# Order in which the moving columns are walked, and their places in SBUF against the weights

## What is computed

```
h = concat(meta, x)                                   # 272 tokens
for l in 0, 1:                                        # first block
    h += 0.5 * swiglu(rmsnorm(h), gate, up, down)     # 1024 -> 2816 -> 1024
    h += hybrid_mixer(rmsnorm(h))                     # w_in 1024 -> 4608, then attention, a 31-tap conv, w_out
    h += 0.5 * swiglu(rmsnorm(h), gate, up, down)
h = rmsnorm(h)[16:]                                   # 256 tokens
for l in 0, 1:                                        # second block
    h += 0.5 * swiglu(rms(h), ...)
    h += differential_attention(rms(h)) if l == 0 else retention(rms(h))
    h += 0.5 * swiglu(rms(h), ...)
```

## Time and profile before

| | |
|---|---|
| median of 2 runs | 2207.22 us |
| the profiled execution | 2210.91 us |
| its span (first to last instruction) | 2209.1 us |
| PE busy | 2198.0 us (99%), 18114 matmuls |
| PEld (weight loads) busy | 2180.8 us (99%), 18114 loads |
| DVE busy | 1602.4 us (73%) |
| ACT busy | 1276.6 us (58%) |
| chain that ended last | PE 98%, ACT 1%, DVE 1% |
| read from HBM | 384.18 MB, 174 GB/s over the span |

### The profile page before, as it was taken

How to read it: one execution, slowest core, us unless ns; L and a number is a source line. 1 busy time by engine, 2 the same in 40 slices (tenths; PEclk the granted TensorE clock), 3 DMA queues, 4 the chain that set the end, 5 groups by cost and what they waited for, 6 DMA issues and landing times.

```text
span 2209.1 us, 48942 instructions
## 1 busy us (share of the span) xinstructions
PE 2198.0 (99%) x18114; PEld 2180.8 (99%) x18114; DVE 1602.4 (73%) x2450; ACT 1276.6 (58%) x1988; POOL 282.1 (13%) x328
## 2 busy tenths in 40 slices
PE   8999999999999999999999999999999999999999
PEld 8999999999999999999999999999999999999999
DVE  6655997665566579887768767888768766777775
ACT  6444786544444368766546646876556645565662
POOL 0001661100100136220020012010010010101000
PEclk9999999999999999999999999999999999999999
DMA  6555435555455544455555555355556645445553
GB/s 229 174 188 165 159 122 170 167 171 195 155 173 183 179 161 144 144 185 186 190 169 193 195 183 163 124 178 194 195 181 200 219 162 177 161 162 194 188 200 124
DMA packets 100408, 386.68 MB, mean 175 GB/s; under 512 B 11312, under 2 KB 12464, under 8 KB 100304
## 3 DMA queue, kind: packets, MB, share of 16 engines
q1 hardware_dynamic: 99648, 383.89, 52.2%
q0 software_dynamic: 368, 1.26, 0.2%
q10 hardware_dynamic: 288, 0.12, 0.0%
HBM read 384.18 MB, written 1.05 MB: 174 GB/s over the span
## 4 chain that ended last, share of the span: by engine, by line
PE 98%; ACT 1%; DVE 1%; issue 0%; DMA 0%; ACTq 0%
PE bank L387 16%; PE bank L389 15%; PE bank L388 15%; PE bank L395 15%; PE bank L396 14%; PE bank L397 14%; PE bank L759 1%; PE bank L1049 1%; PE bank L1050 1%; PE bank L1051 1%; PE bank L1096 0%; PE bank L709 0%; PE bank L740 0%; PE bank L940 0%; PE bank L943 0%; PE bank L942 0%
## 5 line engine op out<-in xcount | busy, mean ns | idle before, releaser
L412 DVE TENSOR_TENSOR wlo<-raw,whi 128x1024 fp32r<-128x1024 f32 (+1 forms) x677 | 893.3, 1322 | 177.8 <-ACT whi L405 165.4
L405 ACT ACTIVATE whi<-raw 128x1024 fp32r<-128x1024 f32 (+1 forms) x677 | 745.5, 1112 | 164.5 <-PE bank L389 117.2
L387 PE MATMUL bank<-u,whi 128*128 128x272 f32 (+1 forms) x1888 | 549.0, 291 | 7.1 <-DVE u L450 7.1
L389 PE MATMUL bank<-u,wlo 128*128 128x272 f32 (+1 forms) x1888 | 543.7, 288 | 0.0
L388 PE MATMUL bank<-u,whi 128*128 128x272 f32 (+1 forms) x1888 | 541.9, 287 | 0.0
L395 PE MATMUL bank<-u,whi 128*128 128x256 f32 x1888 | 529.2, 280 | 0.2
L397 PE MATMUL bank<-u,wlo 128*128 128x256 f32 x1888 | 527.4, 279 | 0.0
L396 PE MATMUL bank<-u,whi 128*128 128x256 f32 x1888 | 527.4, 279 | 0.0
L387 PEld LDWEIGHTS bank<-u,whi 128*128 128x128 f32 x1888 | 356.9, 189 | 8.0 <-DVE wlo L412 7.3
L388 PEld LDWEIGHTS bank<-u,whi 128*128 128x128 f32 x1888 | 357.0, 189 | 0.9 <-issue 0.2
L397 PEld LDWEIGHTS bank<-u,wlo 128*128 128x128 f32 x1888 | 357.6, 189 | 0.0
(11 more groups left out here) (332 smaller groups left out, 3448.8 us busy)
## 6 DMA issues: line engine op xcount, KB each, us to landing
raw<-w SPq DMA_DIRECT2D x552, 512.0 KB, 3.4
raw<-w SPq DMA_DIRECT2D x128, 704.0 KB, 4.1
h<-xT SPq DMA_DIRECT2D x4, 272.0 KB, 4.9
outT<-h SPq DMA_DIRECT2D x8, 128.0 KB, 4.7
consts<-cst POOLq DMA_DIRECT2D x1, 576.0 KB, 4.6
dist<-cst POOLq DMA_DIRECT2D x1, 192.0 KB, 2.7
rdist<-cst POOLq DMA_DIRECT2D x1, 192.0 KB, 3.0
sgain<-small POOLq DMA_DIRECT2D x1, 145.5 KB, 4.8
```

What stands on the lines that cost most here:

```text
L387: pe.matmul(out, w_h, x_hi, start=first, stop=False)
L389: return pe.matmul(out, w_l, x_hi, start=False, stop=last)
L405: act.activation(whi[:, n % RING, 0:COLS[n]], raw[:, n % RING, 0:COLS[n]], ACT.Copy).then_inc(hi_ready, 1)
L412: dve.tensor_tensor(wlo[:, n % RING, 0:COLS[n]], raw[:, n % RING, 0:COLS[n]], whi[:, n % RING, 0:COLS[n]], ALU.subtract).then_inc(lo_ready, 1)
```

## The change

Three things, all in one edit.

The walk. `spread` turns the columns of both operands, moving tile and PSUM output, into a pattern of runs taken by turns from the first and the second half. With 256 columns the order is 0-15, 128-143, 16-31, 144-159, ...; with 272 it is 0-7, 136-143, 8-15, 144-151, .... Every column is still computed once and lands where it did. All calls of `products` and `split_products` get it; the other matmuls do not.

The steps. In the phases 0 to 4 the tiles of an eight-tile panel lie 144 words apart in `whi` and `wlo` (`GAP_STEP`), not 128, and the tiles of `hid` 320 apart (`HID_STEP`), not 272. ACT's and DVE's split write and read `whi` and `wlo` in eight runs of 128 words there. The slot and the DMA into `raw` stay.

The places. `U_PLACE` and `HID_PLACE` give for each phase the distance of the high part, and what the low part has beyond it. `u` grows by 104 words, `hid` to 22 x 2 x 320 + 96.

```diff
-U_PAD, HID_PAD, RY_PAD = 112, 24, 144
+RY_PAD, GAP_STEP, HID_STEP = 40, 144, 320
+U_PLACE = {0: (48, 0), 1: (32, 0), 2: (16, 0), 3: (0, 0), 4: (48, 32), 5: (48, 0), 6: (16, 0), 8: (48, 0), 9: (0, 0), 10: (48, 32), 11: (48, 0), 12: (16, 32), 7: (16, 0)}
+HID_PLACE = {0: (48, 0), 2: (32, 0), 3: (16, 0), 5: (48, 0), 7: (0, 32), 9: (16, 0), 10: (48, 16), 12: (0, 0)}
...
-        u = sb("u", [128, 2 * KD * T], f32r)
+        u = sb("u", [128, 2 * KD * T + 104], f32r)
...
-            hid = sb("hid", [128, 2 * FT * T], f32r, area)
+            hid = sb("hid", [128, 2 * FT * HID_STEP + 96], f32r, area)
...
-        def tile_of(buf, tiles, pad, y, part, k, c0, c1):
-
-            width, first, at = (T, 0, 0) if y <= LAST_MIX else (SEQ, META, pad)
-            at += part * tiles * width
-            parts = buf[:, at:at + tiles * width].rearrange("p (k c) -> p k c", c=width)
+        def tile_of(buf, tiles, step, place, y, part, k, c0, c1):
+
+            first = first_col(y)
+            at = part * tiles * step + sum(place[:part + 1])
+            parts = buf[:, at:at + tiles * step].rearrange("p (k c) -> p k c", c=step)
             return parts[:, k, c0 - first:c1 - first]
 
         def u_at(y, part, k, c0=None, c1=T):
-            return tile_of(u, KD, U_PAD, y, part, k, first_col(y) if c0 is None else c0, c1)
+            return tile_of(u, KD, width(y), U_PLACE[y], y, part, k, first_col(y) if c0 is None else c0, c1)
 
         def hid_at(y, part, f):
-            return tile_of(hid, FT, HID_PAD, y, part, f, first_col(y), T)
+            return tile_of(hid, FT, HID_STEP if y <= LAST_MIX else SEQ, HID_PLACE[y], y, part, f, first_col(y), T)
...
-        def products(pe, out, slot, k, x_hi, x_lo, first, last):
-
-
-            w_h, w_l = whi[:, slot, k * 128:k * 128 + 128], wlo[:, slot, k * 128:k * 128 + 128]
+        def weights(part, n):
+
+            w, tiles = (whi, wlo)[part], COLS[n] // 128
+            step = GAP_STEP if n < BASE[LAST_MIX + 1]["P"] and COLS[n] == K8 else 128
+            return w[:, n % RING, 0:tiles * step].rearrange("p (k c) -> p k c", c=step)[:, :, 0:128]
+
+        def spread(x, run=16):
+
+            return x.rearrange("p (s m e) -> p m s e", s=2, e=run)
+
+        def products(pe, out, n, k, x_hi, x_lo, first, last):
+
+
+            w_h, w_l = weights(0, n)[:, k, :], weights(1, n)[:, k, :]
+            run = 16 if out.shape[-1] == SEQ else 8
+            out, x_hi, x_lo = spread(out, run), spread(x_hi, run), spread(x_lo, run)
             pe.matmul(out, w_h, x_hi, start=first, stop=False)
             pe.matmul(out, w_h, x_lo, start=False, stop=False)
             return pe.matmul(out, w_l, x_hi, start=False, stop=last)
 
-        def split_products(pe, out, slot, k, x_hi, x_lo, first, last):
-
-
-            w_h, w_l = whi[:, slot, k * 128:k * 128 + 128], wlo[:, slot, k * 128:k * 128 + 128]
-            pe.matmul(out[:, 0:SEQ], w_h, x_hi, start=first, stop=False, skip_group_check=True)
-            pe.matmul(out[:, SEQ:2 * SEQ], w_h, x_lo, start=False, stop=last, skip_group_check=True)
-            return pe.matmul(out[:, 0:SEQ], w_l, x_hi, start=False, stop=last, skip_group_check=True)
+        def split_products(pe, out, n, k, x_hi, x_lo, first, last):
+
+
+            w_h, w_l = weights(0, n)[:, k, :], weights(1, n)[:, k, :]
+            hi_out, lo_out = spread(out[:, 0:SEQ]), spread(out[:, SEQ:2 * SEQ])
+            pe.matmul(hi_out, w_h, spread(x_hi), start=first, stop=False, skip_group_check=True)
+            pe.matmul(lo_out, w_h, spread(x_lo), start=False, stop=last, skip_group_check=True)
+            return pe.matmul(hi_out, w_l, spread(x_hi), start=False, stop=last, skip_group_check=True)
...
-                act.activation(whi[:, n % RING, 0:COLS[n]], raw[:, n % RING, 0:COLS[n]],
+                act.activation(weights(0, n), raw[:, n % RING, 0:COLS[n]].rearrange("p (k c) -> p k c", c=128),
                                ACT.Copy).then_inc(hi_ready, 1)
 
...
-                dve.tensor_tensor(wlo[:, n % RING, 0:COLS[n]], raw[:, n % RING, 0:COLS[n]],
-                                  whi[:, n % RING, 0:COLS[n]], ALU.subtract).then_inc(lo_ready, 1)
+                dve.tensor_tensor(weights(1, n), raw[:, n % RING, 0:COLS[n]].rearrange("p (k c) -> p k c", c=128),
+                                  weights(0, n), ALU.subtract).then_inc(lo_ready, 1)
...
-                                mm = split_products(pe, bank[g % 4], n % RING, k, u_at(uy, 0, k),
+                                mm = split_products(pe, bank[g % 4], n, k, u_at(uy, 0, k),
                                                  u_at(uy, 1, k), k == 0, k == KD - 1)
                             else:
-                                mm = products(pe, bank[g % 4][:, 0:N], n % RING, k, u_at(uy, 0, k),
+                                mm = products(pe, bank[g % 4][:, 0:N], n, k, u_at(uy, 0, k),
                                               u_at(uy, 1, k), k == 0, k == KD - 1)
...
-                                mm = split_products(pe, bank[4 + j % 2], n % RING, k, x(0, K), x(1, K), K == 0, K == last)
+                                mm = split_products(pe, bank[4 + j % 2], n, k, x(0, K), x(1, K), K == 0, K == last)
                             else:
-                                mm = products(pe, bank[4 + j % 2][:, 0:N], n % RING, k, x(0, K), x(1, K),
+                                mm = products(pe, bank[4 + j % 2][:, 0:N], n, k, x(0, K), x(1, K),
                                               K == 0, K == last)
...
-                        mm = products(pe, bank[j % MIX_BANKS][:, 0:cols], (P + j) % RING, k, u_at(y, 0, k, T - cols),
+                        mm = products(pe, bank[j % MIX_BANKS][:, 0:cols], P + j, k, u_at(y, 0, k, T - cols),
                                       u_at(y, 1, k, T - cols), k == 0, k == KD - 1)
...
-                                mm = products(pe, bank[g % MIX_BANKS][:, 0:N2], n % RING, 4 * ff + k, x_hi,
+                                mm = products(pe, bank[g % MIX_BANKS][:, 0:N2], n, 4 * ff + k, x_hi,
                                               x_lo, k == 0, k == 3)
...
-                        mm = products(pe, bank[MIX_OUT[f]][:, 0:N2], (P + 44 + f) % RING, k, qk[:, k, W2], qk[:, KD + k, W2],
+                        mm = products(pe, bank[MIX_OUT[f]][:, 0:N2], P + 44 + f, k, qk[:, k, W2], qk[:, KD + k, W2],
                                       k == 0, k == KD - 1)
...
-                        mm = split_products(pe, bank[panel_bank(acc)], (b["P"] + j) % RING, k, u_at(y, 0, k), u_at(y, 1, k),
+                        mm = split_products(pe, bank[panel_bank(acc)], b["P"] + j, k, u_at(y, 0, k), u_at(y, 1, k),
                                              k == 0, k == KD - 1)
                         continue
-                    mm = products(pe, bank[panel_bank(acc)][:, 0:SEQ], (b["P"] + j) % RING, k, u_at(y, 0, k, META),
+                    mm = products(pe, bank[panel_bank(acc)][:, 0:SEQ], b["P"] + j, k, u_at(y, 0, k, META),
                                   u_at(y, 1, k, META), k == 0, k == KD - 1)
```

## The result

The changed kernel takes **2278.48 us** (median of 2, 2277.90 to 2279.06), against 2207.22: the ratio is 1.0323 with a 95% interval of 1.0247 to 1.0398. It is 3.2% slower, where -62 us was forecast.

A forecast was written before the change was run, and what follows sets the result against it. PE's pace of matmul starts was taken as the bound. Terms -94 (gain), +27 (distance 0), +5 (mixers) summed to -62 us, forecasting 2145 us at 50%; 8 in 10 range 2070 to 2265 us.

The forecast's parts named there:

- What bounds the kernel: PE, busy 99% of the span at 2.4 GHz, never short of input; time is matmuls times distance between starts.
- The mechanism: In SBUF, moving and weight reads meet; walked by turns both go equally fast and keep their starting distance, so stay apart.
- the 94 us of gain: Four fifths of the 118 us excess held by the 13280 matmuls off distance 0.
- Distance 0: 3424 matmuls whose two streams start in the same place and stay together: 8 ns each, 27 us lost.
- The gain that could be had: Excess of the 272- and 256-column matmuls above their floors, 144 us if all reached them.
- The floor of 109 ns: Least distance between starts at 256 columns, taken from weight loads following each other at 109 ns.
- The jumps: 15 or 33 address jumps a matmul: taken as zero; as a rival 6.3 or 13.9 ns a matmul, 2299 us, 10%.
- The splits: ACT and DVE writing eight runs of 128 words in phases 0 to 4: taken as zero, 13 us at most.
- DVE in the mixers: DVE is full there, so a faster PE must wait: 5 us of the gain given back.
- The signs: Right: 109 to 111 ns in phases 5, 7; wrong: uniform shift (jumps), 145 ns at 0 (together), old 113 and 118 (nothing).
- Together for good: Rival: streams at distance 0 and 48 share a place and never part; sum +116, 2323 us; 13%.
- The walk does nothing: Rival: excess has another source, paces only drawn again, -14 to +14 us, 2207 us; 15%.

The follow-up runs named there:

- e9: Changed kernel, mostly straight walk, other data; by phase, weight loads read one word 128 times or every second word, some moving reads repeated or by turns: 2233.4 us.
- e3: Changed kernel with only the PSUM output columns walked by turns, moving columns read straight: 2219.9 us.
- e4: Changed kernel with only the moving columns read by turns, output written straight: 2279.8 us.
- e8: Changed kernel with output straight and moving columns read in made-up patterns (jumps in straight order, doubled runs, same 16 words), other data: 2227.5 us.
- e1: Changed kernel with its places and steps, but every product walks its columns straight: 2220.45 us, ratio 1.0062.
- e10: Changed kernel with ten distances by phase, loads reading one word 128 times and moving columns the same 8 words 32 times: 2164.9 us.
- e11: Changed kernel, all places at 48, other data; repeated words, short runs by turns or runs 64 apart, with loads still, double or as ever: 2228.4 us.
- e2: Kernel before with only the walk by turns added, places and steps as before: 2274.15 us, ratio 1.0288.
- e13: Changed kernel at distance 48, other data, the second half of the walk moved to 128 + d words from the first, d varied by phase: 2242.0 us.
- e14: Changed kernel at distance 48, other data, moving columns read as eight runs of 8 words, spacing varied by phase, four times over: 2291.8 us.

## Why the prediction was wrong

*What bounds the kernel: right.* PE at the higher clock, no long waits; the loss is all pace.

*The mechanism: wrong, and this is the step that failed*: "the distance then stays what it was at the start", and with it the 94 us of gain taken for the 13280 matmuls off distance 0. No phase got faster. The walk gave 120.0 ns at 48, 16 and 0 alike, where the straight walk had 117.8 or 113.3, and about 130 at 272 columns, where it had 126; that is 68 us of span lost where 62 were to be won. With a load that reads one word, and so keeps no pace with anything, it is 120.0 as well (e9). I had the excess from one observation, the uneven steps at 272 columns, and took the meeting of two streams for its only source. What the change altered first was the order in which the moving stream visits the address classes modulo 64 words, and this has a price of its own: e3 and e4 put the walk's whole loss into the read, and e8 has the straight pace with as many jumps in straight order.

*Distance 0: wrong in kind.* The 27 us taken for it never came: it is no worse than the other distances under the new walk (u of 3 has 129.4 ns, u of 2 at 16 has 130.4). It costs the straight one (120.1 ns in e1, where 48 had 117.8).

*The gain that could be had: wrong in size.* The floor of 109 ns was reached by no run; the lowest pace was 111.7, for 8 words or fewer read again and again (e10, e11).

*The jumps: right.* Zero for the write (e3) and zero over 117.8 ns for 15, 31 and 63 jumps of the read in straight order (e8, e9). The Trainium skill ("PSUM — Partial Sum Buffer", Specifications) says that any pattern that isn't contiguous slows matmuls significantly; e3 doesn't bear that out for a write in runs of 8 and 16 words: 2219.9 us with it, 2220.45 without.

*The splits: right*, 1250 ns against 1252. *DVE in the mixers:* never called on, as PE got slower; the 5 us for it didn't arise.

*The signs.* The one that came was that of the jumps, all phases shifted and more at 272 than at 256 columns (e2: 3.9 ns and more, against 2.2 where the slower pace had been). It was a poor sign, for the order gives it too; the jumps were priced at 13.9 and 6.3 ns, and e8 and e9 rule them out.

*The rivals.* "Together for good" had the direction, and priced it at 116 us through the places 0 and 48; measured were 71, through all places, and not by a shared one. "The walk does nothing" was right in a side remark: phases 9 and 10 lost their fast pace, 21 of the 68 us, more than the 14 I gave it since they went to 120 and not to 117.8. I should have given the two paces of one and the same code more weight: they were in the earlier trace rows.

*What stays open.* Why by turns costs 2 to 7 ns whatever lies between the halves (e13), while 15 to 63 jumps in straight order cost none; how far the loads take part; and what picks one of the paces for a phase. e14 shows the classes with runs of 8; of runs of 16 only the spacing 64 was run.

## What to carry to other kernels

Where PE is busy throughout, measure starts apart, phase by phase, not busy time: one kernel can give each phase another variant, and ten prices come from one execution. Then repeat what matters in another phase and another execution: here the same code had two paces 4.5 ns apart. Read moving tiles in address order, or in runs whose starts step on in the order of addresses modulo 64 words; not in short runs at multiples of 64 words (24 ns more in runs of 8, 2 ns in runs of 16). Before explaining a pace by two parties, make one of them stand still.

## What was not expected of the hardware

- Runs of 8 words at multiples of 64 words (256 bytes) apart took 141.9 ns for 256 columns, at other spacings 117.8 to 118.9 (e14). The same 8 words over and over took 111.7 (e10, e11).
- Many whole-phase paces lie 3.3 ns apart: 113.3, 116.7, 120.0, 123.3, 126.7, 130.0. Others lie between them, such as 117.8, 118.7, 122.2 and 124.3. 117.8 is a cycle of three matmuls with different steps: in phase 5 of the kernel before 118.3, 117.5 and 117.5 ns ahead of L395, L396 and L397.
- The walk by turns holds one pace: four executions of e2 lie within 0.8 us, where 13 of the kernel before spread over 22.7 us.
- The same code at the same distance runs a whole phase at 113.3 or at 117.8 ns. A phase of 1584 matmuls makes 7.1 us of it, and the executions of the kernel before fall into groups near 2204, 2211, 2218 and 2225 us. So one phase may change its pace from one execution to the next; each kernel has one profiled execution, so this is inferred from the times. A median of two executions, as in the result above, can be off by 3 us for it.
